# A two-block model on one core: casts of the first attention two panels ahead and its products by tiles, the softplus series moved, the last recurrent unit's casts and additions reordered, and the merged H written beside the branches

## The reference

```python
def first_block(x, c, ...):
    for layer in range(2):
        mod = (silu(c) @ mod_w[layer] + mod_b[layer]).reshape(B, 3, 3, 1024)   # shift, scale, gate
        x = x + 0.5 * g * swiglu(h, ffn_w_gu[layer, 0], ffn_w_down[layer, 0])  # f0, f2
        y = stick_breaking_attention(h, w_qkv, w_o) if layer == 0 else rglru_block(h, ...)   # sb, lru
        x = x + g * y
        x = x + 0.5 * g * swiglu(h, ffn_w_gu[layer, 1], ffn_w_down[layer, 1])  # f1, f3
    return rmsnorm(x, final_norm_g)

def rglru_block(h, ...):
    gate, xb = split(h @ w_in)                       # 1280 features each, 10 blocks of 128
    xc = conv4(xb); r = sigmoid(xc @ w_r + b_r); i = sigmoid(xc @ w_i + b_i)
    log_a = -8.0 * r * softplus(-lam)
    hs = scan(exp(log_a), sqrt(-expm1(2 * log_a)) * (i * xc))
    return (gelu(gate) * hs) @ w_out

def hybrid_layer(x, ...):                            # h0, h1
    ya, yb, yc = three attentions of projections of h, each times silu of its gate
    merged = (sigmoid(m_g[0]) * (ya @ w_br_a) + sigmoid(m_g[1]) * (yb @ w_br_b)
              + sigmoid(m_g[2]) * (yc @ w_br_c))
    return x + merged @ w_out
```

## Time and profile before

| | |
|---|---|
| device time, median of 3 runs | 3413.18 us (3405.5 to 3429.3) |
| the profiled execution: own time | 3413.44 us |
| its span, first to last instruction | 3411.6 us |
| mean granted TensorE clock | 0.967 of full speed |
| PE busy | 3226.3 us, 95% of the span |
| DVE, ACT, POOL busy | 52%, 34%, 5% |

### The profile page before, as it was taken

One profiled execution on the slowest core, in us unless ns is written; L12 is line 12 of the kernel. 1 busy time (PEld: TensorE's weight loads), 2 busy tenths in 40 slices (PEclk: granted clock), 3 DMA queues, 4 the chain that ended last, 5 costly groups with the idle time before them and its releaser, 6 DMA issues.

```text
span 3411.6 us, 38726 instructions
## 1 busy us (share of the span) xinstructions
PE 3226.3 (95%) x16353; PEld 2666.2 (78%) x16353; DVE 1769.3 (52%) x2488; ACT 1167.0 (34%) x1526; POOL 166.2 (5%) x228
## 2 busy tenths in 40 slices
PE   6999989999999999999999998889989998899998
PEld 5887877788888888887888887666768886567687
DVE  6555542355555643367633335776643458755434
ACT  4222355542222312247432232233442232335322
POOL 0000011110000000001100000000000010000000
PEclk8999999999999999999999998989989999899899
DMA  5555421125554443231333323221213232222131
GB/s 218 193 177 180 141 75 50 50 73 175 184 186 148 149 148 99 90 112 50 99 99 99 99 74 93 75 62 50 81 50 99 74 104 79 66 62 75 50 99 68
DMA packets 287270, 354.23 MB, mean 104 GB/s; under 512 B 9546, under 2 KB 263290, under 8 KB 287098
## 3 DMA queue, kind: packets, MB, share of 16 engines
q1 hardware_dynamic: 287098, 351.75, 31.8%
HBM read 336.52 MB, written 2.10 MB: 99 GB/s over the span
## 4 chain that ended last, share of the span: by engine, by line
PE 81%; DVE 10%; ACT 6%; issue 1%; POOL 1%; DMA 1%; SPq 0%; DVEq 0%; ACTq 0%; POOLq 0%
PE psum L591 57%; PE psum L730 6%; PE psum L688 3%; PE psum L1152 3%; PE psum L1021 2%; PE psum L612 2%; PE psum L1059 2%; DVE w_low L1725 1%; PE psum L824 1%; PE psum L1037 1%; DVE psum L1874 1%; DVE area L2188 1%; PE psum L557 1%; DVE h_low L1884 1%; PE psum L684 1%
## 5 line engine op out<-in xcount | busy, mean ns | idle before, releaser
L591 PE MATMUL psum<-h_high,w_high 128*128 128x512 f32 (+1 forms) x2496 | 990.0, 397 | 50.9 <-DVE w_low L1725 21.4
L591 PE MATMUL psum<-h_low,w_high 128*128 128x512 f32 (+1 forms) x2496 | 981.7, 393 | 0.0
L591 PE MATMUL psum<-h_high,w_low 128*128 128x512 f32 (+1 forms) x2496 | 980.8, 393 | 0.0
L1725 DVE TENSOR_TENSOR w_low<-raw,w_high 128x2048 fp32r<-128x2048 f32 (+2 forms) x246 | 546.3, 2228 | 307.8 <-ACT w_high L1210 307.6
L1210 ACT CAST w_high<-raw 128x2048 fp32r<-128x2048 f32 (+3 forms) x254 | 464.3, 1840 | 530.9 <-DMA raw<-in_ffn_w_gu 237.1
L591 PEld LDWEIGHTS psum<-h_high,w_high 128*128 128x128 f32 (+1 forms) x2496 | 474.5, 190 | 162.1 <-issue 35.2
L591 PEld LDWEIGHTS psum<-h_high,w_low 128*128 128x128 f32 (+1 forms) x2496 | 474.0, 190 | 101.7
L591 PEld LDWEIGHTS psum<-h_low,w_high 128*128 128x128 f32 (+1 forms) x2496 | 474.7, 190 | 99.0 <-issue 1.0
L591 PE MATMUL psum<-y_high,w_high 128*128 128x512 f32 x592 | 234.0, 395 | 11.2 <-DVE w_low L1725 8.6
L1995 DVE TENSOR_TENSOR area<-area,psum 128x512 f32<-128x512 f32 x88 | 60.2, 684 | 342.4 <-PE psum L591 334.0
L591 PE MATMUL psum<-y_low,w_high 128*128 128x512 f32 x592 | 232.4, 393 | 0.0
(11 more groups left out here) (294 smaller groups left out, 4403.7 us busy)
## 6 DMA issues: line engine op xcount, KB each, us to landing
raw<-in_ffn_w_gu SPq DMA_DIRECT2D x88, 1024.0 KB, 5.9
raw<-in_mod_w SPq DMA_DIRECT2D x64, 1024.0 KB, 5.0
raw<-in_w_in SPq DMA_DIRECT2D x64, 1024.0 KB, 5.2
raw<-in_ffn_w_down SPq DMA_DIRECT2D x32, 1024.0 KB, 7.5
raw<-in_ffn_w_down SPq DMA_DIRECT2D x16, 768.0 KB, 4.9
raw<-in_sb_w_qkv SPq DMA_DIRECT2D x12, 1024.0 KB, 5.2
area<-area SPq DMA_DIRECT2D x92, 128.0 KB, 2.3
raw<-in_lru_w_in SPq DMA_DIRECT2D x10, 1024.0 KB, 5.3
```

Source lines behind the costliest of these rows:

```text
L591: mm = e.matmul(psum[0:width, base + m, :], wv[a][:, at_k, c0:c0 + width], X[b][:, k, :], start=(at_k == 0 and (a, b) == (0, 0)), stop=(at ...
L1725: e.tensor_tensor(w_low[raw_at[m]][:, :n], raw[raw_at[m]][:, :n], w_high[x % NW][:, :n].bitcast(F32), ALU.subtract).then_inc(*q.up(s_low, ...
```

## The change

1. sb: ACT and DVE issue casts and remainders of weight panels two panels ahead (`two_ahead_of`). The products (0, u) and (1, u) run one 128-column tile after the other (`product_tiles`), each bank of the pair is freed by its own tile's copy, and ACT copies by tiles: both tiles of q between the casts `sb_high` of x = 0 and x = 1, both tiles of k behind the weight casts.
2. `decay` moves from f0 to f2, between the gate and up panels of c0 = 12.
3. lru, last unit: ACT's last two panel casts move ahead of exp and tanh (`between`), DVE takes the second small panel ahead of `out`, and the first full panel before the addition of c = 2, which now stands ahead of `power` with nothing between.
4. h0 and h1: a step `h_read` is marked on PE behind the last gate product. ACT casts `merged` from there on as its parts come, and DVE writes the remainders of the first six tiles ahead of the last branch sums and those of the last two behind them.

PE's order of matmuls is the same but for the tile order within the six products of part 1, and SP's is unchanged.

```diff
+            def product_tiles(key, X, x_ready, ks):
+                i, w, total = w_views(*key)
+                take(i)
+                base = base_of[key] = only[0]
+                wv = [x[:, :total].rearrange("p (k n) -> p k n", n=PANEL) for x in w]
+                wait_panel(i)
+                for m in range(2):
+                    wait_free(base + m)
+                    for at_k, k in enumerate(ks):
...
+                        for a, b in COMBOS:
+                            mm = e.matmul(psum[:, base + m, :], wv[a][:, at_k, m * P:(m + 1) * P], X[b][:, k, :],
...
+                    mm.then_inc(*q.up(s_product, "product_tile", *key, m))
...
@@ tensor: stick_breaking, beside
-                    b = product_tokens(key, H, hr, PANEL) if part == 2 else product(key, H, hr, range(KD), PANEL)
-                    free_pair(b, ("qkv", part, u))
+                    b = product_tiles(key, H, hr, range(KD))
+                    for m in range(2):
+                        free[b + m] = [("qkv_tile", part, u, m)]
@@ tensor: hybrid
+                    if jj == KD // 2 - 1:
+                        q.mark("h_read", stage)
@@ scalar and vector: ffn
                             take(gate)
+                            if (stage, c0) == ("f2", 12):
+                                decay()
                             take(up)
-                    if (stage, row) == ("f0", KD):
-                        decay()
@@ scalar: stick_breaking
+                def kept_tile(part, u, m):
...
+                    q.wait_ge(*at("product_tile", *key, m))
...
+                    e.mul((sb_q, sb_k)[part][u % 2][:, m, :], psum[:, base_of.get(key, 0) + m, :], SCALE if part == 0 else 1.0).then_inc(
...
                         e.copy(sb_high[x], sb_sp[x]).then_inc(*q.up(s_act, "sb_high", p, x))
+                        if both and x == 0:
+                            kept_tile(0, u, 0)
+                            kept_tile(0, u, 1)
                     for part, u in SB_BESIDE.get(p, ()):
-                        take((stage, part, u))
-                        kept(part, u)
+                        split_to(two_ahead_of(number[stage, part, u]))
+                        if part == 2:
+                            kept(part, u)
+                    if both:
+                        kept_tile(1, u, 0)
+                        kept_tile(1, u, 1)
@@ scalar: rglru
-                def recur(n0):
+                def recur(n0, between=()):
...
+                    for key in between:
+                        take(key)
...
-                    recur(n0)
+                    recur(n0, () if more else [(stage, "back", 0, 2), (stage, "back", 0, 3)])
...
-                    else:
-                        for c in range(2, NC):
-                            take((stage, "back", 0, c))
@@ scalar: hybrid
-                fence(q, (stage, "merged"))
+                q.wait_ge(*at("h_read", stage))
@@ vector: rglru
+                    else:
+                        take((stage, "back", 0, 0))
...
-                        project_back(stage, 0, x_of(stage), panels_of=range(NC - 1))
+                        project_back(stage, 0, x_of(stage), panels_of=range(2))
+                        take((stage, "back", 0, 3))
+                        project_back(stage, 0, x_of(stage), panels_of=range(2, 3))
@@ vector: hybrid
+                def merged_low(j):
+                    q.wait_ge(*at("h_read", stage))
+                    q.wait_ge(*at("merged_high", stage, j))
+                    e.tensor_tensor(H[1][:, j, :], L.merged[:, j, :], H[0][:, j, :].bitcast(F32), ALU.subtract).then_inc(*q.up(s_vec, "merged_low", stage, j))
...
+                    if jj == KD // 2 - 1:
+                        for j in range(2 * jj):
+                            merged_low(j)
...
-                for j in range(KD):
+                for j in range(KD - 2, KD):
+                    merged_low(j)
```

More of the change, by code:

```diff
@@ L596, in product @@
                 return base
+            def product_tiles(key, X, x_ready, ks):
[7 more added lines that the diff above has]
+                    for at_k, k in enumerate(ks):
+                        for h in range(2):
+                            for step in x_ready(k, h):
+                                q.wait_ge(*at(*step))
+                        for a, b in COMBOS:
+                            mm = e.matmul(psum[:, base + m, :], wv[a][:, at_k, m * P:(m + 1) * P], X[b][:, k, :],
+                                          start=(at_k == 0 and (a, b) == COMBOS[0]), stop=(at_k == len(ks) - 1 and (a, b) == COMBOS[-1]))
+                    mm.then_inc(*q.up(s_product, "product_tile", *key, m))
+                q.mark("w_done", i)
+                return base
             def product_tokens(key, X, x_ready, n):
@@ L788, in beside @@
                     key = (stage, part, u)
-                    b = product_tokens(key, H, hr, PANEL) if part == 2 else product(key, H, hr, range(KD), PANEL)
-                    free_pair(b, ("qkv", part, u))
+                    if part == 2:
+                        free_pair(product_tokens(key, H, hr, PANEL), ("qkv", part, u))
+                        return
+                    b = product_tiles(key, H, hr, range(KD))
+                    for m in range(2):
+                        free[b + m] = [("qkv_tile", part, u, m)]
                 def scores(p):
```

13 lines of the change are left out of this document (11 added, 2 removed).

## The result

| | before | after |
|---|---|---|
| device time, median of 5 runs each | 3413.18 us (3405.5 to 3429.3) | 3380.99 us (3374.72 to 3386.03) |
| span of the profiled execution | 3411.6 us | 3379.6 us |
| mean granted TensorE clock | 0.967 | 0.969 |

The ratio after / before is 0.9899, with a 95% interval of 0.9868 to 0.9931. That is 34 us less (23 to 45), with 42.8 forecast; the two medians differ by 32.2 us and the two profiled executions by 32.0. So the time is 11 us above the forecast of 3370, 1 us above the forecast's own range (3362 to 3380) and inside the range of 8 in 10 (3359 to 3384).

The account below looks back on a forecast made before the run. PE, 95% busy, was taken to lose time to operand waits and slow matmuls behind them; 24.7 + 5.75 + 11.1 + 1.3 = 42.8 us off gave 3370 us, own range 3362 to 3380, 8 in 10 from 3359 to 3384.

Parts of the forecast that it names:

- Reading of the bound: Whole kernel: PE busy 95%, so time comes only from its idle stretches, mostly waits for `w_low` and `h_low`, and slow matmuls.
- Part 1: First attention (sb): earlier casts remove 17.3 us of waits and 7.45 of slow matmuls, 24.7 together, bounds 21 to 26.
- the concern about banks: sb, odd pairs: the pair of banks could be late next; copied by tiles, neither bank makes PE wait.
- tiles in a row into one bank: Rival, sb's six products: 24 matmuls in a row into one bank cost 47 us, time 3417; chance 2%.
- Part 2: decay leaves f0, removing a 3.92 us wait and 1.83 of slow matmuls, and hides in f2: gain 5.75, lower bound 4.
- The table load of 1.28 us: f2: Abs, Exp and two table loads of 1.28 need about 3.0 us, within ACT's 3.87 idle before the Silu.
- Part 3: Ends of h0 and h1: the product behind the branches starts at once; net 5.5 us a layer, 11.1 for both.
- The second panel: h0 and h1 ends: the second panel's remainder ends near 2700.9, PE wants it at 2700.75, a wait of 0.3 us.
- Part 4: Last unit of lru: the `w_low` wait moves to `y_low`, about 4 us; gain 1.3, bounds a loss of 1.5 to a gain of 5.
- 1.5 to 3 us besides: Whole kernel: a PE wait of about 4 us or more costs itself and this much more, as the clock falls.
- H beside the branches gives nothing: Rival, h0 and h1 ends: six remainders delay the sums and the passage to the norm sets the end; 3381.5 us, 13%.
- The clock stays low without the waits: Rival: sb keeps 7.45 us and the ends of h0 and h1 3.1 of slow matmuls; time 3381, 4%.

Follow-up runs that it names:

- 24.8 alone: Kernel before with only the sb edits (casts two panels ahead, products and copies by tiles): 3394.50 us, ratio 0.9931; sb 24.8 us shorter.
- The kernel with whole copies: Kernel after with casts still two panels ahead, but whole products and whole copies of q and k in sb: 3376.99 us, one run.
- the part alone: Kernel before with only decay moved from f0 to f2: 3398.49 us, ratio 0.9938.
- the next pair: Kernel after plus one line behind the heads of h0 and h1 that shifts the turn of PSUM pairs: 3371.91 us, ratio 0.9870.

## Why the prediction was right, and where not

- **Reading of the bound**: right. Waits for `w_low` and `h_low` and the slow products behind them were the time to be had, and where they went, both went: sb, f0 and the end of h1 came out within 0.9 us of the sum.
- **Part 1**: right in size (24.7 forecast, 24.8 alone, 23.9 in after) and in its cover: no product waited for a copy of a tile, and the waits for exponentials are as before (1.9 us in 7). The kernel with whole copies shows that the concern about banks was real, 1.1 us a pair. The rival of tiles in a row into one bank is refuted: 96 matmuls in 21.99 us, 0.229 each.
- **Part 2**: right in its place (5.8, and f2 unchanged); the 21 us by the runs of the part alone were not foreseen and are not explained. The table load of 1.28 us, for which the prediction names, is in none of those rows, which are DVE's; ACT's load ahead of the Exp in f0 does take 1.28.
- **Part 3, the step that failed**: "But PE starts at 2689.85 with k = 0 and needs the seventh tile only 36 matmuls later". The step asked only when H is there, and not when the pair of banks is. For h0's last product the pair is fixed, and it was that of the last branch. The same part had moved the sums 1.6 us back ("the five operations ... end at 2693.9 instead of 2692.3, 1.6 later"), at no cost, it said; in fact the third multiplication released PE. Even unmoved it would have held PE up for about 1.2 us. The prediction's own sign for this, "if the last sums of h0 hold up its second product by more than 2 us", named the wrong product: they held up the first by 2.74. The price is the wait of 2.74 and 12.80 - 10.88 = 1.92 of slow matmuls: 4.7, of which the next pair gave back 4.4 (184.25 - 179.80). For h1, where the pair is another, the step was right to 0.4 us.
- **The second panel** behind H ("a wait of 0.3"): no such wait in h1, where PE has none from its last branch product to the end of the 192 matmuls.
- **Part 4**: the mechanism was right, the wait has moved to `y_low`, and it is 3.57 against "about 4". The loss behind it is not one number: with the part, lru came out at 213.2 to 214.8, and without it at 215.1 to 216.0. That is a gain of 0.3 to 2.8 around the 1.3 forecast; after, at 0.6, had all 12 matmuls slow, 5.44 - 2.77 = 2.7.
- **A term that was missing**: the sum took the clock's losses as fixed for every wait that stays. They are not. The profiled executions differ in the heads of h0 from 509.5 to 526.0 us. After's heads are 6.2 us longer than before's, 4.4 of it in h1 where the clock falls at a wait that stayed, in every kernel with part 3; its f3 is 1.6 shorter. The sum had no term for either. The range of 8 in 10 covered this, the sum could not: the prediction's "1.5 to 3 us besides" was read behind its largest waits, and behind those of 2 to 3.2 us it can be anything from nothing to that.
- **The rivals**: "H beside the branches gives nothing" gave 3381.5, by chance next to the 3381 measured; the part did give 7 of its 11 us, and its reason, that the passage to the norm sets the end, is not what the trace shows: the product's start set h0's end. "The clock stays low without the waits" is refuted: without the wait the products of sb, f0 and h1 take 10.9 to 11.0.

## What to carry to other kernels

When a product is freed from waiting for its operand, ask at once for the second thing that it needs, its PSUM banks: write down which instruction empties them, on which engine, and whether the edit itself pushes that instruction back. A count of buffers that is fixed by hand at a seam (here one pair for the passage) deserves that check first, and mending it may be one line. And cast weights further ahead before reordering anything finer: the two-panel lead alone was worth four fifths of the largest gain.

## What the runs showed of the hardware that was not expected

- Behind equal PE waits of 2 to 3.2 us the granted clock either held at 1.00 or fell to 0.50, with 0.1 to 2.7 us of loss each time. At one of them (2.27 us, in h1) it held in all four kernels without H beside the branches and fell in all eight with it, some 55 us behind the edited end of h0: so an edit seems able to cost something in a piece that it doesn't touch. Kernels that differ from after by a few tiny instructions at the start have spans of 3376.9 and 3388.7 against 3379.6. Changes worth less than that can't be judged by one profiled execution's span; its untouched stages have to be taken out first.
- A wait of 1.1 us for a bank left the clock alone (11.17 us for 48 matmuls), three times out of three in sb.
- A DVE remainder of 128 by 512 took 2.47 us instead of 0.68 while a POOL multiplication of 2.40 ran beside it: nearly a full stop until POOL was done. Begun 0.17 us ahead of POOL's, another kept its 0.67 and POOL's took 2.74.
